# Start-up of a two-layer pooling and retention trunk: the adaLN stream opens the queue, and the second norm's transposes move ahead of its column

## The chip, the cores and the metric

One Trainium2 chip, one core. The metric is device microseconds of one execution. The kernel before takes 2433.22 us, the median of 3 runs (2433.15 to 2435.69).

## The reference, cut to what matters

x is 256 tokens by 2048 channels; everything is float32. There are two layers. Each has a mixer (causal pooling in layer 0, retention in layer 1) and a squared-ReLU MLP with 8192 hidden channels. In front of each of these four stands an RMSNorm whose result is scaled and shifted by rows that are computed from the conditioning vector c, and behind each a gate row computed in the same way. These rows are called adaLN rows here.

```python
cond = jax.nn.silu(c)
for i in range(DEPTH):
    mod = jnp.einsum('bd,sdk->bsk', cond, ada_w[i]) + ada_b[i]
    shift_t, scale_t, gate_t = jnp.split(mod[:, 0], 3, axis=-1)
    shift_m, scale_m, gate_m = jnp.split(mod[:, 1], 3, axis=-1)
    h = modulate(rmsnorm(x, norm_g[i, 0]), shift_t, scale_t)
    ...
    x = x + gate_t[:, None, :] * y
    h = modulate(rmsnorm(x, norm_g[i, 1]), shift_m, scale_m)
    x = x + gate_m[:, None, :] * sq_relu_mlp(h, mlp_w1[i], mlp_w2[i])
return rmsnorm(x, final_g)
```

## The kernel before, in words

Five engines run their own programs, written out by hand in the order in which each executes them, and meet in semaphores. Every large load is issued by SP, in order, on one queue. A load that has to wait for its buffer holds back all that stand behind it.

**adaLN pieces.** The weights of the adaLN rows come in pieces of 128 rows by 1024 columns (512 KB). A segment is 32 pieces: segments 0, 1 and 2 are shift, scale and gate of the pooling mixer, segment 3 is the lower half of shift and scale of the first MLP, segment 4 the upper half. Pieces 0 to 15 of a segment make its first 1024 columns and pieces 16 to 31 the other 1024. Segments 0 to 4 use 12 buffers in turn (`ada_raw` 4, `ada_early_h` or `ada_early_a` 8), so piece n may be loaded once piece n-12 has been used. A table says who uses a piece (`ON_PE`): the DVE multiplies it by its column of `cond` and adds it to `ada_acc` (L1346, L1349), or TensorE multiplies it into a PSUM bank (L689). In front of the last piece of each sixteen, TensorE adds what the DVE has summed (`row_blocks`, L664) and waits for `ada_done` to do so.

**From a segment to a norm.** The ACT copies the bank to `seg_row` (L1082), TensorE transposes it to columns (`column`, L747), the DVE adds the bias (L1446) and makes the gain (L1606). The normed x of the first MLP comes from TensorE: `norm_fill(f)` (L785) multiplies two of the 16 channel blocks of x by a diagonal matrix of the tokens' inverse root mean squares, which transposes and scales them at once, into bank `tb`. There are eight fills. `norm_evac` (L1017, called from `norm_bank`) evacuates one with gain and shift into a small buffer `hbuf`, and the DVE splits it into `h_hi` and `h_lo` (`split_h`, L1617 and L1619).

**The products.** Each float32 product is made of three passes: weights are split by the ACT into `w_hi` (L972, `hi`) and by the DVE into `w_lo` (L1340, `lo`). A chunk is 256 rows by 512 columns of weights (512 KB, four buffers), 12 matmuls of 128x512 on TensorE (L555). Here the first MLP starts with 28 chunks (`p1`, seven parts of four) that need only the lower half of the normed x, while segment 4 is still being loaded, and goes on with the upper half (`h1`).

**Order of the work around the change.** SP: eight small tables (c, norm gains, identity, four of biases, `rcount`), four pieces, x, then pieces, with pool weights and two MLP chunks in between (behind pieces 25 and 27 of segment 3), then two more chunks, then chunks and segment 4's pieces in turn. The ACT queue issues `bias_row` and `scale_row` first, each one row copied to 128 partitions. POOL loads the MLP's gate bias (a row of 2048 copied to 128 partitions, 1 MB written) as soon as x holds the mixer's result. TensorE makes fills 0 and 1 behind piece 15 of segment 3, and fills 2 to 7 each ahead of a chunk of the MLP.

## Time and profile before

| | before |
|---|---|
| timed runs | 2433.22 us (2433.15 to 2435.69) |
| profiled execution's own time | 2431.67 us |
| its span | 2429.8 us |
| TensorE busy | 2347.9 us, 97% |
| VectorE (DVE) busy | 1573.0 us, 65% |
| ScalarE (ACT) busy | 1082.4 us, 45% |
| mean of the DMA | 256 GB/s |

The span runs from the first instruction to the last; the execution's own time is 1.9 us longer. Times in all rows are microseconds from the span's start. TensorE's busy share says that most of the span is matmuls. Its first twelfth is another stage: there the DMA engines are busy all the time and TensorE is not. The change lies in that stage and at its end.

### The profile page before, as it was taken

How to read it: one execution, taken by the hardware profiler on the slowest of the kernel's cores; microseconds unless marked ns; L12 is line 12 of the kernel's file. 1: busy time of each engine (PE TensorE's matmuls, PEld its weight loads, DVE VectorE, ACT ScalarE, POOL GpSimd, SP SyncE). 2: the span in 40 equal slices, each digit the busy share in tenths (PEclk: the TensorE clock that was granted, in tenths of full speed). 3: DMA queues.
4: the chain of work that ended last, by engine and by line, in shares of the span. 5: the costliest groups of instructions: out<-in, count | busy, mean ns of one | idle time of the engine just before them, and what ended most of it. 6: DMA issues, size and time to landing. Idle time of an engine off the chain costs nothing.

```text
span 2429.8 us, 30034 instructions
## 1 busy us (share of the span) xinstructions
PE 2347.9 (97%) x10421; PEld 1857.0 (76%) x10421; DVE 1573.0 (65%) x1646; ACT 1082.4 (45%) x1346; POOL 21.7 (1%) x30
## 2 busy tenths in 40 slices
PE   5778999999999999999999999999999999999998
PEld 1235788888888887888888888887788888888886
DVE  4567787676676888657566656566876444445455
ACT  1323454443443545444444444455543443443443
POOL 0000000000000000000000000000000000000000
PEclk8789999999999999999999999999999999999999
DMA  9999889887887986766766766666987656656654
GB/s 369 406 392 373 323 291 326 300 291 251 292 301 254 321 318 201 263 220 224 229 212 226 248 212 225 219 224 198 330 289 239 186 186 192 185 187 194 187 182 155
DMA packets 269404, 620.89 MB, mean 256 GB/s; under 512 B 19064, under 2 KB 19400, under 8 KB 268360
## 3 DMA queue, kind: packets, MB, share of 16 engines
q1 hardware_dynamic: 268112, 612.65, 74.6%
q0 software_dynamic: 880, 5.77, 0.7%
q8 instruction: 90, 1.47, 0.2%
q10 hardware_dynamic: 264, 0.52, 0.1%
q14 instruction: 58, 0.48, 0.1%
HBM read 616.77 MB, written 2.10 MB: 255 GB/s over the span
## 4 chain that ended last, share of the span: by engine, by line
PE 91%; DMA 4%; DVE 3%; issue 1%; ACT 1%; SPq 1%; POOL 0%; ACTq 0%; POOLq 0%; DVEq 0%
PE acc L555 85%; DMA ada_early_h<-in_ada_w 3%; PE tb L656 2%; PE mod_ps L689 1%; PE score_ps L689 1%; DVE ada_acc L1346 0%; DMA ada_raw<-in_ada_w 0%; DVE w_lo L1340 0%; PE score_ps L906 0%; PE tb L785 0%; SPq L399 0%; DVE h_lo L1534 0%; PE mod_ps L664 0%; PE score_ps L664 0%; PE acc L916 0%
## 5 line engine op out<-in xcount | busy, mean ns | idle before, releaser
L1340 DVE TENSOR_TENSOR w_lo<-raw,w_hi 128x1024 fp32r<-128x1024 f32 x776 | 947.0, 1224 | 735.3 <-ACT w_hi L972 735.2
L972 ACT ACTIVATE w_hi<-raw 128x1024 fp32r<-128x1024 f32 x776 | 822.0, 1060 | 1167.8 <-PE acc L555 1096.8
L555 PE MATMUL acc<-w_hi,h_lo 128*128 128x512 f32 x1792 | 706.4, 394 | 8.6 <-DVE h_lo L1534 5.7
L555 PE MATMUL acc<-w_hi,h_hi 128*128 128x512 f32 x1792 | 698.0, 390 | 0.0
L555 PE MATMUL acc<-w_lo,h_hi 128*128 128x512 f32 x1792 | 697.4, 389 | 0.0
L555 PE MATMUL acc<-w_hi,a_lo 128*128 128x512 f32 x1312 | 516.5, 394 | 0.0
L555 PE MATMUL acc<-w_hi,a_hi 128*128 128x512 f32 x1312 | 511.1, 390 | 0.0
L555 PE MATMUL acc<-w_lo,a_hi 128*128 128x512 f32 x1312 | 510.7, 389 | 0.0
L555 PEld LDWEIGHTS acc<-w_hi,h_lo 128*128 128x128 f32 x1792 | 336.5, 188 | 86.3 <-issue 7.9
L555 PEld LDWEIGHTS acc<-w_hi,h_hi 128*128 128x128 f32 x1792 | 336.4, 188 | 70.5
L555 PEld LDWEIGHTS acc<-w_lo,h_hi 128*128 128x128 f32 x1792 | 336.7, 188 | 68.8 <-issue 1.4
L1346 DVE SCALAR_TENSOR_TENSOR ada_acc<-ada_raw,cond,ada_acc 128x1024 f32<-128x1024 f32 x238 | 304.3, 1279 | 17.0 <-DMA ada_raw<-in_ada_w 16.8
L555 PEld LDWEIGHTS acc<-w_hi,a_lo 128*128 128x128 f32 x1312 | 246.6, 188 | 60.2 <-issue 8.5
L555 PEld LDWEIGHTS acc<-w_lo,a_hi 128*128 128x128 f32 x1312 | 246.7, 188 | 52.2 <-issue 1.9
L555 PEld LDWEIGHTS acc<-w_hi,a_hi 128*128 128x128 f32 x1312 | 246.4, 188 | 51.9
L988 ACT ACTIVATE ev<-acc 128x512 f32<-128x512 f32 x121 | 64.6, 584 | 7.7 <-PE acc L555 6.4
L1346 DVE SCALAR_TENSOR_TENSOR ada_acc<-ada_early_h,cond,ada_acc 128x1024 f32<-128x1024 f32 x36 | 46.2, 1284 | 32.4 <-DMA ada_early_h<-in_ada_w 32.1
L1582 DVE TENSOR_TENSOR a_lo<-tb,a_hi 128x512 fp32r<-128x512 f32 x80 | 51.3, 682 | 0.0
L689 PE MATMUL mod_ps<-ada_early_h,cond 128*32 128x512 f32 x88 | 31.6, 814 | 17.9 <-DMA ada_early_h<-in_ada_w 17.9
L1003 ACT ACTIVATE sq_junk<-x 128x512 bf16<-128x512 f32 x46 | 28.4, 618 | 35.1 <-DVE x L1495 16.8
L993 ACT ACTIVATE a_hi<-tb 128x512 fp32r<-128x512 f32 x80 | 42.7, 586 | 0.0
L1227 ACT ACTIVATE ev<-ev 128x512 f32<-128x512 f32 x64 | 36.7, 627 | 0.0
(162 smaller groups left out, 759.2 us busy)
## 6 DMA issues: line engine op xcount, KB each, us to landing
raw<-in_mlp_w SPq DMA_DIRECT2D x512, 512.0 KB, 4.4
ada_raw<-in_ada_w SPq DMA_DIRECT2D x280, 512.0 KB, 5.8
raw<-in_ret_w_in SPq DMA_DIRECT2D x192, 512.0 KB, 3.9
ada_early_h<-in_ada_w SPq DMA_DIRECT2D x84, 512.0 KB, 13.1
raw<-in_ret_w_out SPq DMA_DIRECT2D x64, 512.0 KB, 4.1
ada_early_a<-in_ada_w SPq DMA_DIRECT2D x20, 512.0 KB, 9.9
raw<-in_pool_w SPq DMA_DIRECT2D x8, 512.0 KB, 12.5
x<-in_x SPq DMA_DIRECT2D x2, 1024.0 KB, 11.3
```

The lines of the kernel that those rows point to most:

```text
L555: mm = nc.tensor.matmul(acc[pair][t][:], l[:, CK * c + j, tok], w[:, c % RING, j, :], start=first and j == 0 and i == 0, stop=last and j = ...
L656: tr = nc.tensor.transpose(tb[b][:, j * S + t * P:j * S + (t + 1) * P], source(t)[:, m * P:(m + 1) * P], ident[:])
L689: mm = nc.tensor.matmul(bank[32 * b:32 * b + 32, :], cond[:, k:k + 1].to_broadcast([P, 32]), raw_rows[:, b % 2 * NB:(b % 2 + 1) * NB], sta ...
L972: nc.scalar.activation(w_hi[:, o % RING], raw[:, o % RING], ACT.Copy).then_inc(hi_ready, 1)
L988: nc.scalar.activation(target[:, t, :], acc[pair][t][:], func).then_inc(evac, 1)
L993: nc.scalar.activation(targets, tb[b][:].rearrange("p (k t) -> p k t", k=2), ACT.Copy).then_inc(tevac, 1)
L1003: nc.scalar.activation(sq_junk[:, t, :], x[:, t, block_ * NB:(block_ + 1) * NB], ACT.Square, accum_out=ssq[:, t, block_:block_ + 1]).then_ ...
L1227: nc.scalar.activation(ev[:, u % 2, t, :], ev[:, u % 2, t, :], ACT.Square).then_inc(sq_done, 1)
L1340: nc.vector.tensor_tensor(w_lo[:, o % RING], raw[:, o % RING], w_hi[:, o % RING].bitcast(F32), ALU.subtract).then_inc(lo_ready, 1)
L1346: nc.vector.scalar_tensor_tensor(out=part, in0=raw_rows, scalar=cond[:, k:k + 1], in1=part, op0=ALU.mult, op1=ALU.add).then_inc(ada_done, 1)
L1582: nc.vector.tensor_tensor(a_lo[:, k:k + 2, :], tb[b][:].rearrange("p (k t) -> p k t", k=2), a_hi[:, k:k + 2, :].bitcast(F32), ALU.subtract ...
```

## The change

Six edits.

1. SP no longer issues the small tables. Its queue opens with the first four adaLN pieces. The ACT queue issues the tables, in the order c, identity, then behind the silu of c: `rcount`, norm gains, four of biases, the two gate rows. TensorE and the DVE take c first (`cond`), and norm gains and biases some pieces later.
2. `bias_row` and `scale_row` are zeroed by POOL and loaded as 4 rows of 512 on partitions 0, 32, 64 and 96, not copied to 128.
3. All eight fills of the MLP's norm stand ahead of its column, between pieces 15 and 24 of segment 3. The ACT copies each bank as it is to scratch (`transposed_x`), in two new buffers `xT`. Gain and shift are applied later, in place: channel blocks 0 and 1 by the DVE (`modulate_first`), the others by the ACT (`norm_bank`).
4. Who uses a piece changes in segment 3: in its first sixteen TensorE has 11 pieces for 9, in the other sixteen 5 for 9.
5. One MLP chunk is loaded within segment 3 (behind piece 29) for two, and the three others of the first four behind its end.
6. POOL's load of the gate bias waits until the upper half of the norm has been split (`h_ready`), since `xT` lies where it lands.

```diff
-LAST_PE = (1, 3, 5, 7, 9, 11, 13, 14, 15)
+LOW_SHIFT_PE = (1, 3, 4, 5, 7, 8, 9, 11, 12, 13, 15)
+LOW_SCALE_PE = (1, 3, 7, 11, 15)
...
+        xT = [scratch[:, 0:2048].rearrange("p (k t) -> p k t", k=KT // 2),
+              scratch[:, 6144:8192].rearrange("p (k t) -> p k t", k=KT // 2)]
...
-                if a in (25, 27):
-                    load_chunk(a // 2 - 12, first_part(a // 2 - 12))
+                if a == 29:
+                    load_chunk(0, first_part(0))
...
             pe.wait_ge(gate_ready, 4)
-            norm(2)
-            shared_rows(3, 16, SEG)
+            pe.wait_ge(diag_ready, 1)
+            for f in range(KT // 2):
+                norm_fill(f)
+                if f % 2:
+                    shared_rows(3, 15 + f, 17 + f)
+            shared_rows(3, 24, SEG)
             column(score_ps)
...
+            def transposed_x(f):
 
                 act.wait_ge(tr_done, n.of("TB") + 1)
+                k = 2 * f % (KT // 2)
+                nc.scalar.activation(xT[f // 4][:, k:k + 2, :], tb[f % 2][:].rearrange("p (k t) -> p k t", k=2),
+                                     ACT.Copy).then_inc(tevac, 1)
...
-            act.dma_start(bias_row[:], by_block(gate_bias)).then_inc(bias_in, 16)
...
+            act.wait_ge(rows_zero, 1)
+            act.dma_start(rows[0:KT, 1, :], c_in.rearrange("b (k p) -> (b k) p", p=P)).then_inc(cond_in, 16)
+            act.dma_start(ident[:], ident_in).then_inc(const_in, 16)
+            act.wait_ge(cond_in, 16)
             nc.scalar.activation(rows[:, 1, :], rows[:, 1, :], ACT.Silu).then_inc(cond_rows, 1)
+            act.dma_start(rcount[:], rcount_in).then_inc(rcount_loaded, 16)
...
+            act.dma_start(bias_row[0:P:32, :], gate_bias.rearrange("(b n) -> b n", b=4)).then_inc(bias_in, 16)
...
+            for f in range(KT // 2):
+                transposed_x(f)
             hi(0)
+            copy_rows(score_ps, 2, PE_BEFORE[4 * SEG])
+            norm_bank(1)
             hi(1)
-            copy_rows(score_ps, 2, PE_BEFORE[4 * SEG])
-            norm_bank(0)
-            norm_bank(1)
+            norm_bank(2)
             hi(2)
-            norm_bank(2)
+            norm_bank(3)
             hi(3)
...
             lo(0)
-            lo(1)
             take_half(0)
             gains(slice(0, KT // 2))
+            modulate_first()
             split_h(0)
             split_h(1)
+            lo(1)
+            split_h(2)
             lo(2)
...
-            pool.wait_ge(x_added, 4 * TT)
+            pool.wait_ge(h_ready, CH)
             load_gate_bias(mlp_gate, 1, mlp_bias_in)
```

The instruction order shows three places. First SP's opening, before:

```order
L452 DMA rows<-in_c 16x128 [waits rows_zero]
L453 DMA rows<-in_norm_g 64x128
L454 DMA ident<-in_ident 128x128
L457 DMA rows<-in_ada_b 32x128 x4
L458 DMA rcount<-in_rcount 128x64
L399 DMA ada_raw<-in_ada_w 128x1024 x4
```

and now, where L407 is the line of the pieces' loads:

```order
L407 DMA ada_raw<-in_ada_w 128x1024 x4
L462 DMA x<-in_x 128x2048 x2
L407 DMA ada_early_h<-in_ada_w 128x1024 x8
L407 DMA ada_raw<-in_ada_w 128x1024 [waits ada_done]
L407 DMA ada_raw<-in_ada_w 128x1024 [waits ada_rows_multiplied]
```

The pieces stand first and wait for nothing. Second, TensorE at the end of segment 3, from its last piece on, before (L747 is the column, L785 a fill, L555 the first MLP chunk):

```order
L689 MATMUL score_ps<-ada_early_h,cond 32x512 [waits ada_in7]
L689 MATMUL score_ps<-ada_early_h,cond 32x512
L747 MATMUL score_ps<-ident,seg_row 128x128 [waits mod_col_ready,seg_row_ready]
L747 MATMUL score_ps<-ident,seg_row 128x128 x3
L785 MATMUL tb<-diag,x 128x128 [waits tr_bank_evacuated,lo_ready]
L785 MATMUL tb<-diag,x 128x128 x3
L555 MATMUL acc<-w_hi,h_lo 128x512 [waits evac_done,h_ready]
```

and now, from fills 6 and 7 (L783) on, with pieces 23 and 27, the sum of the DVE's share (L662) and piece 31 ahead of the column (L745):

```order
L783 MATMUL tb<-diag,x 128x128 [waits tr_bank_evacuated]
L783 MATMUL tb<-diag,x 128x128 x3
L687 MATMUL score_ps<-ada_early_h,cond 32x512 [waits ada_in11]
L687 MATMUL score_ps<-ada_early_h,cond 32x512
L687 MATMUL score_ps<-ada_raw,cond 32x512 [waits ada_in3]
L687 MATMUL score_ps<-ada_raw,cond 32x512
L662 MATMUL score_ps<-ada_acc,ones 32x512 [waits ada_done]
L662 MATMUL score_ps<-ada_acc,ones 32x512
L687 MATMUL score_ps<-ada_early_h,cond 32x512 [waits ada_in7]
L687 MATMUL score_ps<-ada_early_h,cond 32x512
L745 MATMUL score_ps<-ident,seg_row 128x128 [waits mod_col_ready,seg_row_ready]
L745 MATMUL score_ps<-ident,seg_row 128x128 x3
```

No fill stands between the column and the MLP's chunks any more. Third, the DVE behind the column (L1446), before:

```order
L1340 TENSOR_TENSOR w_lo<-raw,w_hi 128x1024 [waits hi_ready] x2
L1446 TENSOR_TENSOR mod_col<-score_ps,bias_col 128x2x8 [waits col_transposed]
L1606 SCALAR_TENSOR_TENSOR gain_col<-mod_col,norm_col 128x8 [waits mod_col_ready]
L1617 CAST h_hi<-scratch 128x512 [waits tr_bank_evacuated]
L1619 TENSOR_TENSOR h_lo<-scratch,h_hi 128x512 [waits h_hi_done]
```

and now:

```order
L1340 TENSOR_TENSOR w_lo<-raw,w_hi 128x1024 [waits hi_ready]
L1446 TENSOR_TENSOR mod_col<-score_ps,bias_col 128x2x8 [waits col_transposed]
L1606 SCALAR_TENSOR_TENSOR gain_col<-mod_col,norm_col 128x8 [waits mod_col_ready]
L1617 TENSOR_SCALAR scratch<-scratch,gain_col,mod_col 128x256 [waits tr_bank_evacuated,gain_ready]
L1617 TENSOR_SCALAR scratch<-scratch,gain_col,mod_col 128x256
L1630 CAST h_hi<-scratch 128x512 [waits first_two_modulated]
L1632 TENSOR_TENSOR h_lo<-scratch,h_hi 128x512 [waits h_hi_done]
```

One of two splits of weights has moved from in front of the column to behind the second split of h, and the DVE applies the first gain and shift itself.

## Rows read from the trace of the kernel before

**Rows 1.** The page: span, and DMA's busy tenths in 40 slices of 61 us.

```profile
span 2429.8 us, 30034 instructions
...
DMA  9999889887887986766766766666987656656654
```

**Rows 2.** Busy time by stage: length, engines, granted clock, DMA share, GB/s.

```profile
0.00:5.00 5.00, 0.00 (x0) 0.00 (x0) 0.00 (x0) 1.28 (x1) 0.81 (x7) 1.00 0.23 65
5.00:10.00 5.00, 0.00 (x0) 0.00 (x0) 0.00 (x0) 0.31 (x1) 0.00 (x0) 1.00 0.84 247
...
175.00:180.00 5.00, 2.99 (x8) 0.55 (x8) 4.13 (x8) 0.36 (x2) 2.32 (x2) 0.50 0.93 322
195.00:200.00 5.00, 4.74 (x12) 1.06 (x14) 2.58 (x3) 0.00 (x0) 0.00 (x0) 0.52 1.04 397
240.00:260.00 20.00, 20.00 (x89) 15.62 (x88) 16.11 (x14) 9.09 (x11) 0.00 (x0) 1.00 1.04 399
```

**Rows 3.** Timeline of the opening: start, length, engine, line, and idle time before.

```profile
1.19 0.39 SPq L452 DMA_DIRECT2D rows<-in_c  x1
5.25 1.96 SPq L399 DMA_DIRECT2D ada_raw<-in_ada_w  x4
6.51 0.31 ACT L1096 ACTIVATE rows<-rows 128x128 f32<-128x128 f32 x1 [2.70 <-DMA rows<-in_norm_g]
...
17.04 0.75 DVE L1349 TENSOR_SCALAR ada_acc<-ada_raw,cond 128x1024 f32<-128x1024 f32 x1
20.18 0.63 ACT L1003 ACTIVATE sq_junk<-x 128x512 bf16<-128x512 f32 x1 [13.36 <-DMA x<-in_x]
```

**Rows 4.** Timeline, TensorE on pieces 5 and 7 of segment 0.

```profile
22.77 1.92 PE L689 MATMUL mod_ps<-ada_early_h,cond 128*32 128x512 f32 x4 [5.62 <-DMA ada_early_h<-in_ada_w]
25.32 1.92 PE L689 MATMUL mod_ps<-ada_early_h,cond 128*32 128x512 f32 x4 [0.63 <-DMA ada_early_h<-in_ada_w]
```

**Rows 5.** Timeline of segment 3: piece 14, SP, the DVE's sum, POOL's load, fills, piece 30.

```profile
168.01 1.05 PE L689 MATMUL score_ps<-ada_raw,cond 128*32 128x512 f32 x4 [0.23 <-DMA ada_raw<-in_ada_w]
164.41 11.62 SPq L399 DMA_DIRECT2D ada_early_h<-in_ada_w  x8
177.01 1.92 PE L664 MATMUL score_ps<-ada_acc,ones 128*32 128x512 f32 x4 [7.95 <-DVE ada_acc L1346]
177.47 0.69 POOL L1955 DMA_DIRECT2D scratch<-in_ada_b  x1
180.57 3.06 PE L785 MATMUL tb<-diag,x 128*128 128x128 f32 x16
196.54 0.13 PEld L689 LDWEIGHTS score_ps<-ada_early_h,cond 128*32 128x32 f32 x2 [1.09 <-DMA ada_early_h<-in_ada_w]
```

**Rows 6.** Timeline from segment 3's row to the MLP's first chunk.

```profile
201.22 0.60 ACT L1082 ACTIVATE seg_row<-score_ps 128x512 f32<-128x512 f32 x1 [7.48 <-PE score_ps L689]
204.48 0.69 DVE L1619 TENSOR_TENSOR h_lo<-scratch,h_hi 128x512 fp32r<-128x512 f32 x1
205.73 1.03 ACT L1017 ACTIVATE scratch<-tb,mod_col,gain_col 128x256 f32<-128x256 f32 x2
205.23 0.50 PE L555 MATMUL acc<-w_hi,h_lo 128*128 128x512 f32 x1
```

**Rows 7.** Chain that ended last, through the MLP's first chunks: start, length, what.

```profile
217.31 1.11 PE tb L785 x8
218.42 2.75 PE acc L555 x12
...
222.15 1.09 PE tb L785 x8
...
297.21 0.89 PE tb L785 x8
```

**Rows 8.** Timeline of the DVE: fourth split of h, fifth split of weights.

```profile
210.28 0.43 DVE L1617 CAST h_hi<-scratch 128x512 fp32r<-128x512 f32 x1 [0.71 <-ACT scratch L1017]
215.99 1.22 DVE L1340 TENSOR_TENSOR w_lo<-raw,w_hi 128x1024 fp32r<-128x1024 f32 x1
```

More of the change, by code:

```diff
@@ L575, in unit, with half_unit @@
                     n.unit(kind)
-            def half_unit(kind, pair, before, after, c0, free):
+            def half_unit(kind, pair, after, c0, free):
                 for o in range(HALF):
                     pe.wait_ge(lo_ready, n.of("U") * HALF + (o + 1))
-                    for hook in before.get(o, []):
-                        hook()
                     ready_h(c0 + o)
@@ L845, in _ @@
             for i in range(PARTS):
-                before, after = {}, {}
-                if i < 2:
-                    before = {o: [lambda f=2 * i + o + 2: norm_fill(f)] for o in range(2)}
+                after = {}
                 for o in range(HALF):
@@ L877, in group @@
                             elif part_of(layer, first, u) is not None:
-                                before = {}
-                                if (first, u) == (0, 0):
-                                    before = {o: [lambda f=6 + o: norm_fill(f)] for o in range(2)}
-                                half_unit("h1", u % 2, before, hooks, HALF, last_but_one if first == 0 else mlp_free(u))
+                                half_unit("h1", u % 2, hooks, HALF, last_but_one if first == 0 else mlp_free(u))
                             elif u < 4:
```

127 lines of the change are left out of this document (68 added, 59 removed).

## The prediction

> **What bounds the kernel now.** First the page. The span is 2429.8 us, and the DMA engines are full in the first four slices and half to three quarters busy later [rows 1]. Then busy time by stage: from 240 us on TensorE is busy 20.00 of 20 us [rows 2]. So behind the start-up every microsecond of the chain is TensorE's, and what the change does there counts only where it takes work from TensorE. Ahead of it the chain waits for pieces. Two pieces that TensorE multiplies one after the other, with one of the DVE's between, are 2.55 us apart [rows 4]: 1.28 us for each 512 KB, 410 GB/s. From about 8 us until the last piece of segment 3 the queue sets the pace, then a chain of small steps leads to the MLP's first chunk at 205.23 us [rows 6]. The time of the kernel is the moment of that chunk plus what TensorE does behind it. The change has four terms, each a shift of one part of this.
>
> **1. The opening.** SP issues c at 1.19 us and the first piece only at 5.25 us [rows 3]; now the piece is issued where the wait on POOL's zeroes used to begin, at about 0.75 us, the issue 4.5 us sooner. The DMA engines have a share of 0.23 in the first 5 us and 0.84 in the next [rows 2], and x, 4 pieces' and 2 MB's worth of transfers behind SP's first load, has landed at 20.18 us [rows 3]. Up to there the engines gave 0.23 x 5 + 0.84 x 5 + 10.2 = 15.5 us, of which the two gate rows copied to 128 partitions (2 x 256 KB) are 1.3. The remaining 14.2, less the 3% by which a full share exceeds 1, is 13.8; it now starts near 2.3 us and ends near 16.1. That is 4.1 us sooner, and I take 4.2. The small tables now compete with the stream instead of standing ahead of it, which is in the 13.8. Bounds: 3.0 if they hold the engines a microsecond longer, 5.5 if most of them are as cheap as their bytes. Who uses the first pieces must keep up: the silu comes 5.3 us after the issue of c, and the DVE takes piece 0 at 17.04 us, 10.5 behind the silu [rows 3]; in these 10.5 lie a wait for tables and, about half, band arithmetic that needs `rcount`, which is now issued behind the silu. With the silu at 4.5 to 6 us and the same 10.5 behind it, piece 0 is taken at 15 to 16.5. The 12 buffers and x (12 x 1.28 + 5.1 from 2.3 on) keep the engines busy until about 23 us, so there are 6 to 8 us of cover.
>
> At the first row a rule of the Trainium skill can be weighed ("DMA: Bandwidth & Descriptors", section "Issuing engines are not separate DMA queues"): loads issued from several engines run on the same 16 engines and interleave, and only the sequencer's issue time is saved. By it this term would be the 4.5 us of issue and the sum 15.1 instead of 14.8.
>
> **2. Segment 3** (times here without the shift of term 1). Piece 14 has landed at 168.01 us and piece 30 at 196.54 [rows 5]: 28.5 us for 16 pieces and two chunks, which at 1.28 us are 23.0. The other 5.5 us are two things. POOL's gate bias at 177.47 us [rows 5] writes 1 MB, two pieces' worth, 2.6 us. And SP needs 11.62 us for eight pieces from 164.41 us on [rows 5], because pieces 4, 6, 8 and 10 are freed by the DVE, one between each two gated blocks of x; the engines run dry (0.93 and 322 GB/s in 175 to 180 us [rows 2]), 2.9 us. All three go. The bias leaves the stage. One chunk, 1.3 us, moves behind piece 31, where it has 6 us before TensorE needs it. TensorE takes pieces 4, 8 and 12, so only 6 and 10 stand between gated blocks: pieces 16 to 25 can be issued by about 168 us and keep the queue full until 182. Piece 30 then comes 17 transfers, 21.8 us, behind piece 14: 6.7 us sooner.
>
> What could block SP now is TensorE, whose fills are in front of pieces 17, 19 and 23. Two cold fills take 3.06 us [rows 5]. The DVE is done with piece 14 3.1 us sooner than with 12 before (two pieces less on its path, no waiting for the last square), so the sum of its share starts near 173.9 instead of 177.01 and the fills near 177. Piece 17 is used by 181, piece 19 by 184 to 185, the last fill ends by 188; pieces 29 and 31 wait for the first two and have backlog until 186 and 190. This is why I take the full term. Bounds: 3.8 (bias and chunk alone) and 7.2.
>
> **3. From piece 30 to the row.** Before: 196.54 to 201.22, 4.7 us [rows 5, 6]. Now piece 30 is the DVE's, 1.28 us, and then come the sum and piece 31 on TensorE. Cold they take 180.57 - 177.01 = 3.6 us [rows 5], at full clock half, 1.8. So 3.2 to 4.9: a gain of 1.5 to a loss of 0.2. The granted clock is 0.52 in 195 to 200 us [rows 2], in a stretch before which TensorE had little; with the fills it has more work, until about 189, but only two pieces in the last 8 us. I take a gain of 0.5, nearer cold.
>
> **4. From the row to the end.** The first h_lo starts at 204.48, lasts 0.69 and is followed by the first matmul at 205.23 [rows 6]. In its chain the ACT's 1.03 us for two blocks [rows 6] becomes two DVE operations of 256 columns, estimated at 0.5 from a 0.75 us operation of 1024 columns [rows 3]: 0.5 sooner. Then the fills leave TensorE: those before chunks 1 and 4 (0.89 and 1.11), 5 (1.09) and the one at 297.21 (0.89) [rows 7]; the other two lay beside the DVE's split. But chunk 4 needs the DVE's fifth w_lo. Before it started at 215.99 [rows 8] and chunk 4 at 218.42, behind the fill [rows 7]. Now one more w_lo (1.13 from start to start) stands in that order, the pause of about 0.8 in front of the fourth split [rows 8] and 0.5 of modulation go: 215.8, ready at 217.0. TensorE would be there at 215.7 and stalls 1.3 us. Chunk 4 gains 1.4, and with 1.09 and 0.89 the term is 3.4. Later the DVE needs 2.5 us a chunk (one w_lo and 1.1 pieces at 1.2) against TensorE's 2.75 [rows 7] and 0.16 of pieces, and does not fall behind again. Bounds: 2.1 (a stall again at chunk 5 or a cold first chunk) and 4.7 (no stall).
>
> The eight plain copies on the ACT, each at most the 1.03 us of two blocks [rows 6], lie beside TensorE's pieces. The gate bias lands near 290 us, long before the last unit of the MLP's first round reads it, while the engines are 7 to 8 tenths busy [rows 1]. Neither costs anything; without cover the load would be 2.6 us.
>
> **Sum.** 4.2 + 6.7 + 0.5 + 3.4 = 14.8 us. The span goes to 2415.0, the profiled execution's own time to 2416.9. The median of the runs is 1.55 above that of the profiled one (2433.22 against 2431.67), so 2418.4 us. The bounds sum to 8.8 and 18.9: 2414.3 to 2424.4.
>
> **The rivals.** *The clock.* TensorE idles before the row and the MLP starts at half speed. What is cold at 0.50 to 0.52 takes twice as long; the first chunk's 2.85 us would be 5.7, of which the 1.3 of stall hide as much, and term 3 is a loss of 0.2: 2.3 us worse, 2420.7. For it, the clock before; against it, the fills. *Fills hold the queue.* If the diagonals come 5 us later than I reckon, SP waits for pieces 17 and 19 and the dry time returns in another place: term 2 is 3.8, the time 2421.3. *Late setup.* If c and `rcount` each take 12 us behind the stream, the band arithmetic (half of the 10.5 us) ends near 31, and the engines stand 9 to 10 us: 2428. Against this the Trainium skill has a rule (the same page, section "Queues, rings and completion order"): each engine takes turns between the queues that have work. No row here shows two full queues at once. *The other side:* the same mechanism at its worst. The kernel is slower only when the DVE's first piece comes 20 us later than the backlog allows, which needs more than 16.6 us for each of the two loads one after the other; at 18 us each it is 2436 to 2438. In the trace x, queued behind four pieces, took 13 us. *No gain in term 4,* the MLP's start being held by weights: 2421.8.
>
> **How the numbers follow.** Forecast 0.50, clock 0.14, fills 0.14, term 4 0.07, late setup 0.10, slower 0.03, and 0.02 for a gain above 19 us. Within 0.2% (4.9 us, about what a measurement can tell) are the worse half of late setup, 0.05, so faster 0.92, same 0.05, slower 0.03. The range runs from the lower bound with a little for the forecast's own error, 2413.5, to 2425.5, which leaves out most of late setup.
>
> **What would show it.** Piece 0 issued under 1 us, x landed near 16; the DVE's piece 0 near 15; pieces 16 to 25 of segment 3 issued without 3 us gaps; the MLP's first matmul near 193.3 (205.23 - 4.2 - 6.7 - 0.5 - 0.5); a stall of TensorE ahead of chunk 4 on w_lo; no L785 row behind the column. The prediction is wrong if the DMA share falls below 1.0 between 15 and 190 us, or if segment 3's last piece waits for TensorE.

## The result and the profile after

The changed kernel takes 2422.12 us (median of 5 runs, 2419.99 to 2422.18), the kernel before in the same session 2434.18 us (median of 5): a ratio of 0.9947, with a 95% interval of 0.9932 to 0.9961, 12.06 us less. The forecast was 14.8 us less, 2418.4 us. The profiled executions are 9.5 us apart (spans 2429.8 and 2420.3).

To see where the time went, two moments are compared in every kernel below: when ACT copies the row of segment 3, which ends the stage that waits for transfers, and when TensorE begins the first transposes of the MLP's activations, which every kernel here reaches by the same work behind the row, but for what was changed. In the kernel before the second moment is this row of the timeline (start, length):

```profile
314.28 0.92 PE L656 MATMUL tb<-ident,ev 128*128 128x128 f32 x7
```

and in the changed kernel this one:

```profile
303.11 1.03 PE L654 MATMUL tb<-ident,ev 128*128 128x128 f32 x8
```

That is 11.17 us sooner. The page of the changed kernel answers to [rows 1]:

```profile
span 2420.3 us, 30026 instructions
...
DMA  9999988887887986776766766766987666666654
```

The busy time by stage answers to [rows 2] (start and end, length, then busy time of PE, PEld, DVE, ACT and POOL with the number of instructions, granted clock, DMA share, GB/s):

```profile
0.00:5.00 5.00, 0.00 (x0) 0.00 (x0) 0.00 (x0) 1.34 (x2) 1.73 (x9) 1.00 0.61 201
5.00:10.00 5.00, 2.62 (x7) 0.74 (x9) 0.17 (x1) 0.25 (x1) 0.00 (x0) 1.00 1.05 420
175.00:180.00 5.00, 5.00 (x35) 3.08 (x34) 4.86 (x5) 1.87 (x4) 0.00 (x0) 1.00 1.03 407
195.00:200.00 5.00, 5.00 (x17) 3.87 (x17) 4.93 (x8) 4.26 (x7) 0.00 (x0) 0.69 0.79 259
280.00:285.00 5.00, 3.07 (x11) 2.12 (x10) 3.31 (x6) 4.94 (x9) 0.00 (x0) 0.85 0.59 224
285.00:290.00 5.00, 5.00 (x20) 4.05 (x19) 3.02 (x5) 2.28 (x4) 0.00 (x0) 0.81 0.64 210
```

The transfers start sooner (0.61 and 1.05 in the first two windows, where 0.23 and 0.84 stood), and the dry stretch of segment 3 is gone (1.03 and 407 GB/s at 175 to 180 us, where it was 0.93 and 322). But behind the row TensorE has two stretches below its full clock, 0.69 at 195 to 200 us and 0.85 and 0.81 at 280 to 290 us. The timeline of the opening answers to [rows 3]:

```profile
0.74 1.83 SPq L407 DMA_DIRECT2D ada_raw<-in_ada_w  x4
1.20 0.40 ACTq L1084 DMA_DIRECT2D rows<-in_c  x1
4.94 0.31 ACT L1087 ACTIVATE rows<-rows 128x128 f32<-128x128 f32 x1 [1.55 <-DMA rows<-in_c]
12.48 0.17 DVE L1653 MEMSET scratch<- 128x128 f32 x1 [4.74 <-DMA rcount<-in_rcount]
14.43 0.63 ACT L998 ACTIVATE sq_junk<-x 128x512 bf16<-128x512 f32 x1 [9.18 <-DMA x<-in_x]
17.50 0.75 DVE L1349 TENSOR_SCALAR ada_acc<-ada_raw,cond 128x1024 f32<-128x1024 f32 x1
```

x is there at 14.43 us instead of 20.18. The DVE's piece 0 at 17.50 is not sooner but 0.46 later. The timeline of segment 3 and of what follows answers to [rows 5, 6]:

```profile
159.49 5.10 SPq L407 DMA_DIRECT2D ada_early_h<-in_ada_w  x8
186.15 1.28 DVE L1346 SCALAR_TENSOR_TENSOR ada_acc<-ada_early_h,cond,ada_acc 128x1024 f32<-128x1024 f32 x1 [1.31 <-DMA ada_early_h<-in_ada_w]
190.85 0.60 ACT L1072 ACTIVATE seg_row<-score_ps 128x512 f32<-128x512 f32 x1 [5.00 <-PE score_ps L687]
...
194.63 0.68 PE L555 MATMUL acc<-w_hi,h_lo 128*128 128x512 f32 x1 [2.47 <-issue]
205.68 1.22 DVE L1340 TENSOR_TENSOR w_lo<-raw,w_hi 128x1024 fp32r<-128x1024 f32 x1
```

SP issues its eight pieces in 5.10 us and not 11.62. Piece 30, now the DVE's (186.15), comes 10.4 us sooner than before, the row 10.37, the MLP's first matmul 10.60. The chain that ended last answers to [rows 7] (start, length, what):

```profile
192.16 2.47 issue
194.63 15.49 PE acc L555 x60
...
277.23 0.44 PE score_ps L745 x4
277.67 2.75 PE acc L555 x12
280.41 1.93 issue
282.35 20.92 PE acc L555 x84
```

No fill stands in it any more. In their place are 60 matmuls in 15.49 us, which at the pace of the 12 in 2.75 us would take 13.8, and at 280.41 us a wait of 1.93 us behind the second column, in front of 84 matmuls that take 20.92 us and not 19.3. So from the row to the transposes only 0.8 us is gained (113.06 us before, 112.26 now), although all the fills left.

Of the 11.17 us the profiled execution shows 1.7 less at its end. One piece of that is a gap in the second round of the MLP, where neither code nor order changed: the chain there reads `601.40 0.84 issue`. The medians, 12.06 us apart, don't show such a loss, and I count it to the scatter of single executions.

### The profile page after: what moved, and what is told of

It is laid out like the page before. It is cut to its first block, busy times and chain, and to the rows that moved or that the text cites. A ratio compares the mean times of both kernels' runs of the same rounds, so it can differ in the third digit from the quotient of the medians.

```text
span 2420.3 us, 30026 instructions
## 1 busy us (share of the span) xinstructions
PE 2343.5 (97%) x10413; PEld 1857.8 (77%) x10413; DVE 1576.8 (65%) x1650; ACT 1087.0 (45%) x1352; POOL 22.2 (1%) x32
## 4 chain that ended last, share of the span: by engine, by line
PE 91%; DMA 4%; DVE 3%; issue 1%; ACT 0%; SPq 0%; POOL 0%; ACTq 0%; POOLq 0%; DVEq 0%
PE acc L555 85%; DMA ada_early_h<-in_ada_w 3%; PE tb L654 2%; DMA ada_raw<-in_ada_w 1%; PE mod_ps L687 1%; DVE w_lo L1340 1%; DVE ada_acc L1346 1%; PE score_ps L901 0%; DVE h_lo L1534 0%; PE mod_ps L662 0%; DMA raw<-in_ret_w_in 0%; DMA rcount<-in_rcount 0%; PE score_ps L687 0%; PE acc L911 0%; PE acc L912 0%
## 5 line engine op out<-in xcount | busy, mean ns | idle before, releaser
L555 PE MATMUL acc<-w_hi,h_lo 128*128 128x512 f32 x1792 | 707.3, 395 | 14.6 <-issue 7.8
L555 PE MATMUL acc<-w_hi,h_hi 128*128 128x512 f32 x1792 | 699.1, 390 | 0.0
L555 PE MATMUL acc<-w_lo,h_hi 128*128 128x512 f32 x1792 | 698.8, 390 | 0.0
L555 PE MATMUL acc<-w_hi,a_lo 128*128 128x512 f32 x1312 | 516.6, 394 | 0.0
L555 PE MATMUL acc<-w_hi,a_hi 128*128 128x512 f32 x1312 | 511.2, 390 | 0.0
L555 PE MATMUL acc<-w_lo,a_hi 128*128 128x512 f32 x1312 | 511.0, 389 | 0.0
L555 PEld LDWEIGHTS acc<-w_hi,h_lo 128*128 128x128 f32 x1792 | 337.2, 188 | 94.0 <-issue 15.6
L555 PEld LDWEIGHTS acc<-w_hi,h_hi 128*128 128x128 f32 x1792 | 337.1, 188 | 70.8
L555 PEld LDWEIGHTS acc<-w_lo,h_hi 128*128 128x128 f32 x1792 | 337.4, 188 | 69.2 <-issue 1.4
L555 PEld LDWEIGHTS acc<-w_hi,a_lo 128*128 128x128 f32 x1312 | 246.6, 188 | 60.4 <-issue 8.6
L555 PEld LDWEIGHTS acc<-w_lo,a_hi 128*128 128x128 f32 x1312 | 246.7, 188 | 52.4 <-issue 1.9
L555 PEld LDWEIGHTS acc<-w_hi,a_hi 128*128 128x128 f32 x1312 | 246.5, 188 | 51.9
```

The source lines that it names most:

```text
L555: mm = nc.tensor.matmul(acc[pair][t][:], l[:, CK * c + j, tok], w[:, c % RING, j, :], start=first and j == 0 and i == 0, stop=last and j = ...
```

## The experiments

Twelve kernels, each timed 5 or 11 times with the kernel before beside it. The changed kernel was timed in another session than they were, and the medians of the kernel before differ by up to 1 us between sessions, so a difference of that size between two medians of this table says nothing. The moments are in us of each profiled execution; "row to transposes" is their difference.

| kernel | median | ratio, 95% interval | row copied | first transposes | row to transposes |
|---|---|---|---|---|---|
| before | 2433.2 to 2434.2 | 1 | 201.22 | 314.28 | 113.06 |
| changed | 2422.12 | 0.9947 (0.9932 to 0.9961) | 190.85 | 303.11 | 112.26 |
| 1 opening only | 2428.50 | 0.9980 (0.9971 to 0.9989) | 195.69 | 308.82 | 113.13 |
| 2 gate bias later only | 2430.42 | 0.9989 (0.9980 to 0.9998) | 198.53 | 311.62 | 113.09 |
| 3 segment 3 only | 2429.70 | 0.9986 (0.9977 to 0.9995) | 196.38 | 310.80 | 114.42 |
| 4 all but the fills | 2423.72 | 0.9961 (0.9947 to 0.9974) | 190.37 | 304.78 | 114.41 |
| 5 column sooner | 2417.17 | 0.9934 (0.9920 to 0.9947) | 190.49 | 298.83 | 108.34 |
| 6 extra matmuls | 2420.72 | 0.9945 (0.9932 to 0.9959) | 190.21 | 302.83 | 112.62 |
| 7 the same, fifth w_lo first | 2418.90 | 0.9939 (0.9925 to 0.9953) | 190.50 | 302.41 | 111.91 |
| 8 rcount sooner | 2420.04 | 0.9945 (0.9932 to 0.9959) | 189.80 | 301.96 | 112.16 |
| 9 as 7, extra matmuls fitted | 2416.43 | 0.9931 (0.9918 to 0.9945) | 189.80 | 298.83 | 109.03 |
| 10 as 9, column sooner | 2413.36 | 0.9917 (0.9904 to 0.9931) | 189.61 | 296.48 | 106.87 |
| 11 wide gate rows on ACT | 2430.54 | 0.9986 (0.9977 to 0.9995) | 199.95 | 311.85 | 111.90 |
| 12 wide gate rows on SP | 2430.53 | 0.9988 (0.9979 to 0.9997) | 197.62 | 309.68 | 112.06 |

### 1 to 4. The parts of the change one by one

My theory was that the terms of the sum stand apart from each other and that the last of them, the fills, had been eaten by the clock. The rival was that one full queue hides or moves part of the gains.

The first takes over the hunks of the diff on the opening alone (SP's first loads, the tables on ACT's queue, the gate rows as 4 rows, the transposes in two steps):

```diff
-            sp.wait_ge(rows_zero, 1)
-            sp.dma_start(rows[0:KT, 1, :], c_in.rearrange("b (k p) -> (b k) p", p=P)).then_inc(rows_in, 16)
...
             for a in range(RING):
                 load_early(0, a)
```

> The kernel before with the opening of the change alone (SP starts with pieces, the tables on ACT's queue, gate rows as 4 rows). My theory: the 4.2 us of term 1 arrive whole and stay, as every later transfer waits in one full queue: x 5.6 us sooner, the copy of the MLP's row by ACT at 197.0 us instead of 201.22, the kernel 4 us faster. Rival 1: part of the changed kernel's gain at the opening belongs to later parts; then the row is copied at 198.5 or later. Rival 2: the segment 3 is bound by SP, which waits for the DVE, and not by bytes; the DVE runs the same steps 4.2 us sooner, so this one also gives 197.0, but the windows from 170 to 185 us would then have no share below 1.

The row comes at 195.69 us, 5.53 sooner, and the median is 4.7 us lower. The gain arrives whole and stays, but it is larger than my term. Not all of it is the opening's: in the chain the last wait for a transfer ends at 190.44 us and not at 195.26, 4.8 us sooner, and the other 0.7 is TensorE's steps from there to the row, 5.3 us where the kernel before took 6.0, with nothing changed in them (the sum alone took 0.86 us, 1.37 before). The dry time is still there, also in this run (0.93 and 318 GB/s at 170 to 175 us), so it was not swallowed by it.

The second is the kernel before with one line changed:

```diff
-            pool.wait_ge(x_added, 4 * TT)
+            pool.wait_ge(h_ready, CH)
             load_gate_bias(mlp_gate, 1, mlp_bias_in)
```

> The kernel before with POOL's 1 MB load of the MLP's gate bias moved behind the MLP's h, and nothing else. My theory: its bytes are worth 2.6 us of a full queue, and the dry time behind the gated blocks stays as it is: row copied at 198.6 us instead of 201.22, DMA share still below 1 in 170 to 185 us. Rival: SP, held by the DVE, was the bound there, and the bias only filled the hole that SP leaves; then the share falls further in that stretch and the row comes less than 1 us sooner.

The row comes 2.69 us sooner, the bytes' 2.6. That the two agree so closely is luck in part: in this execution the DVE's first gated block of x came 0.7 us later than before (162.62 and 161.90 us), and TensorE's steps behind the last wait for a transfer took 0.5 us less, with nothing changed in either. The stretch stays dry, as the busy time by stage of this run shows (columns as above):

```profile
175.00:180.00 5.00, 2.27 (x6) 0.56 (x8) 4.13 (x8) 1.08 (x4) 1.68 (x1) 0.50 0.92 324
180.00:185.00 5.00, 5.00 (x26) 2.97 (x23) 4.58 (x4) 0.00 (x0) 0.00 (x0) 0.69 0.95 313
```

So the bias and SP's wait for the DVE are two separate losses.

The third adds to the second the table of pieces, the DVE's order and the chunk behind piece 29:

```diff
+PE_OF = [EARLY_PE] * 6 + [LOW_SHIFT_PE, LOW_SCALE_PE] + [LATE_PE] * 2
...
-                if a in (25, 27):
-                    load_chunk(a // 2 - 12, first_part(a // 2 - 12))
+                if a == 29:
+                    load_chunk(0, first_part(0))
...
-            early(3, 4, 6)
+            early(3, 4, 8)
             gated(1)
-            early(3, 6, 8)
+            early(3, 8, 11)
             gated(2)
-            early(3, 8, 10)
             gated(3)
```

> The kernel before with the three changes to segment 3: which pieces TensorE takes and the DVE's order around the gated blocks, one chunk behind piece 29 where two stood at 25 and 27, the gate bias later. Fills and opening as before. My theory: the whole of term 2, 6.2 us (piece 30 at 190.3, row copied at 195.0), of which 2.6 are in the run with the bias alone. Rival: the order of the DVE and TensorE gives nothing by itself, because the dry time is refilled by backlog later; then the row is copied at about 197.3 (bias and chunk, 3.9).

First a line of its busy time by stage, then its piece 30 in the timeline of the DVE:

```profile
175.00:180.00 5.00, 5.00 (x24) 2.99 (x20) 4.34 (x7) 0.00 (x0) 1.15 (x1) 0.66 1.02 406
```

```profile
191.34 1.28 DVE L1348 SCALAR_TENSOR_TENSOR ada_acc<-ada_early_h,cond,ada_acc 128x1024 f32<-128x1024 f32 x1 [1.30 <-DMA ada_early_h<-in_ada_w]
```

The queue is full now (406 GB/s), and piece 30 comes at 191.34, 5.2 us sooner than the 196.54 of before [rows 5]. That is more than the bias's 2.7 and less than the 6.2 expected of this run and the 6.7 of the forecast. The row is only 4.84 us sooner and the transposes only 3.48: with more of TensorE's pieces at the front of the segment, it has less to do at its end, and the granted clock is 0.59 and 0.50 in 185 to 195 us. The steps behind piece 30 take 5.04 us (4.7 before), and 1.36 us more go by from the row to the transposes. The chain shows where these are. The fill behind the column takes 1.83 us and not 1.13, and the first chunk 3.66 and not 2.98. This is the chunk in the kernel before and in this run:

```profile
205.26 2.98 PE acc L555 x12
...
201.13 3.66 PE acc L557 x12
```

The granted clock in 200 to 205 us is 1.00 in the kernel before and 0.70 here. In the kernel before and in runs 1 and 2 the first chunk runs at full clock; in the changed kernel and in runs 3, 4, 5, 8, 11 and 12, all with the new order of segment 3 and without extra matmuls, it does not. So the cold start of the MLP comes with the new order of segment 3 and not with the fills.

The fourth is the changed kernel without the hunks on the fills (the function `norm` back, `hbuf` in place of `xT`, no `modulate_first`):

```diff
-            for f in range(KT // 2):
-                norm_fill(f)
-                if f % 2:
-                    shared_rows(3, 15 + f, 17 + f)
+            norm(2)
+            shared_rows(3, 16, SEG)
```

> The changed kernel without its fills ahead: opening and segment 3 as changed, but the second norm's fills, the ACT's modulation and the DVE's split as before (two fills ahead of the column, the others in front of chunks 1 and on). My theory: the row is copied at 190.9 as in the changed kernel, or up to 0.7 later since TensorE has less work ahead of it; TensorE's first chunk is 0.3 to 0.5 us later behind the row; and the fills cost their 4 us in the MLP's first round but hide the clock's loss and the idle of 1.93 us at the second column, so that the first transposes of the MLP come at 316 (changed: 315.05): the fills' removal is worth 1 us and not 3.4. Rival: it is worth the 3.4 of term 4, what the changed kernel lost to the clock having another cause, and the transposes come at 318.4.

Row at 190.37, transposes at 304.78. Against this run the changed kernel needs 2.15 us less from the row to the transposes, where I had said 1 us here and 3.4 in the forecast. This is not yet what the fills are worth at like clocks: both kernels start the first chunk cold, but only the changed kernel also has the 0.85 and 0.81 behind the second column (this run: 1.00 from 280 to 300 us). And against the kernel before both runs with the new segment 3 and the old fills (3 and 4) need 1.35 us more behind the row, which is the cold start again (here the fill takes 2.05 us and the first chunk 3.43). Together, 2.15 - 1.35 is the 0.8 us of the changed kernel.

### 5. The second column sooner

```diff
-                    after[HALF - 2] = [lambda: column(score_ps)]
+                    after[HALF - 3] = [lambda: column(score_ps)]
...
-                    if (i, s) == (PARTS - 1, HALF - 1):
+                    if (i, s) == (PARTS - 1, HALF - 2):
                         take_half(1)
```

and one step sooner on ACT as well (`copy_rows`, `norm_bank(4)`, `norm_bank(5)`).

> The changed kernel with the MLP's second column one chunk sooner on TensorE (behind chunk 1 of the last part and not behind chunk 2), the copy of its row one chunk sooner on ACT, and column, gains, modulation and split one chunk sooner on DVE and ACT. My theory: the 1.93 us for which TensorE waits at 280.41 us are the way from the column to the first split, behind a w_lo that the DVE takes first, and the granted clock of 0.85 and 0.81 in 280 to 290 us follows from that idle time: both go, 1.93 + 1.6 us, the first transposes of the MLP come at 299.6 us instead of 303.11. Rival 1: the clock falls there for a reason of its own; then only the idle goes, 301.2. Rival 2: TensorE then waits for the weights of the next chunk instead, and no more than 0.5 us is gained.

The chain that ended last, behind the second column:

```profile
274.02 0.44 PE score_ps L745 x4
274.46 24.53 PE acc L555 x108
298.99 0.87 PE tb L654 x8
```

In this chain of run 5 108 matmuls follow the column in one stretch at full clock, and the way from the row to the transposes is 3.92 us shorter (3.5 expected). The median falls by 5 us. The wait and the low clock behind it are gone together, as in my theory, but runs 9 and 11 below show that the second does not always follow the first.

### 6, 7 and 9. Keeping TensorE's clock

```diff
+            def keep_warm(count):
+                for _ in range(count):
+                    nc.tensor.matmul(acc[0][0][:, 0:S], ones[:], x[:, 0, 0:S], start=True, stop=True)
...
-            shared_rows(3, 24, SEG)
+            shared_rows(3, 24, SEG - 1)
+            pe.wait_ge(evac, 4 * TT)
+            keep_warm(8)
+            shared_rows(3, SEG - 1, SEG)
+            keep_warm(3)
             column(score_ps)
+            keep_warm(8)
```

> The changed kernel with 19 matmuls of 128x256 on TensorE whose result nobody reads, 8 ahead of the last sum of segment 3, 3 behind its last piece, 8 between the column and the first chunk of the MLP. My theory: they keep the clock at its full level, the row's two steps take 1.7 us instead of 3.4 and the row is copied at 189.4 us instead of 190.85, and the first chunk takes 2.85 us instead of 4.4. But then chunk 4 stands for 1.2 us for the DVE's fifth w_lo, as term 4 of the prediction had it, and of the 3.0 us 1.8 are left: first transposes at 301.3 instead of 303.11. Rival 1: no stall at chunk 4, 300.1. Rival 2: the clock does not come back for them, and nothing is gained or 0.5 us lost.

The granted clock is 1.00 in every window from 180 to 205 us, but the eight matmuls ahead of the sum take 3.65 us and not the 1.8 that I had reckoned, and the sum and the first chunk wait for them: first matmul at 195.15, 0.5 later than without. The row is copied at 190.21 us and the transposes come at 302.83, where 189.4 and 301.3 were expected. And the stall of term 4 appears. In the chain of this run chunk 4 hangs on the DVE's fifth w_lo:

```profile
203.02 1.29 DVE ada_acc L1356
204.38 1.17 issue
205.55 1.23 DVE w_lo L1350
206.82 3.01 PE acc L555 x12
```

The next run lets the DVE take that w_lo first:

```diff
             for i in range(PARTS):
                 for s in range(HALF):
+                    if (i, s) == (0, 0):
+                        lo(s + LEAD)
                     early(4, late_pieces(HALF * i + s + LEAD - 1), late_pieces(HALF * i + s + LEAD))
```

> The kernel of the run with the extra matmuls, and the DVE takes its fifth w_lo ahead of the four pieces of segment 4 that stand in front of it. My theory: the fifth w_lo is ready by 201 us, the stall ahead of chunk 4 goes, and the first transposes come at 300.1 us, 1.2 us sooner than without. Rival: chunk 5 or 6 then waits, since the four pieces stand in front of the sixth w_lo; then the two runs are within 0.4 us.

The transposes come at 302.41 us, not at 300.1. From the row to the transposes this run needs 0.71 us less than run 6, between the 1.2 and the 0.4 of the two views. The stall existed, and was smaller than I had said (about 0.7 us, since run 6 began its first chunk 0.5 us late). Then the counts are fitted, 4, 1 and 5 in place of 8, 3 and 8:

> The kernel with the extra matmuls and the fifth w_lo taken first, with 4, 1 and 5 extra matmuls in place of 8, 3 and 8: each lasted 0.46 us and not the 0.23 that I had reckoned, so that 8 of them pushed the sum of segment 3 back by 1 us and the first chunk by 1 us. My theory: the clock stays full and nothing is pushed back; from the DVE's piece 30 (186.15 in the changed kernel) the row is copied 3.2 us later and not 4.7, the first chunk begins at 193.2 us and is warm, and the first transposes come at 299.8 us instead of 303.11. Rival: with fewer matmuls the clock falls as in the changed kernel; then 302 to 303.

The transposes come at 298.83 us, 4.28 sooner than in the changed kernel where 3.3 was expected, and the median is 5.7 us lower. In the chain of this run:

```profile
193.58 13.86 PE acc L555 x60
...
277.76 1.91 issue
279.67 19.32 PE acc L555 x84
```

The first 60 matmuls take 13.86 us instead of 15.49: the cold start had cost 1.63 us. Behind the wait of 1.91 us, which is as long as before, 84 matmuls take 19.32 us instead of 20.92, at a clock of 1.00 (changed kernel: 0.85 and 0.81):

```profile
280.00:285.00 5.00, 5.00 (x23) 4.10 (x22) 4.02 (x5) 4.31 (x8) 0.00 (x0) 1.00 0.51 147
285.00:290.00 5.00, 5.00 (x24) 4.14 (x23) 3.71 (x6) 2.12 (x2) 0.69 (x1) 1.00 0.94 276
```

Nothing was changed there. Run 11 below, which has no extra matmuls and a cold first chunk, shows the same:

```profile
290.77 1.91 issue
292.69 19.33 PE acc L555 x84
```

So the same wait of 1.90 to 1.93 us costs 1.6 us more in five executions (the changed kernel and runs 6, 7, 8 and 12, 84 matmuls in 20.91 to 20.93 us) and nothing more in two (runs 9 and 11). Not all that run 9 gains is then owed to the extra matmuls. The 1.63 us at the first chunk are: without them the 60 matmuls took 15.31 to 16.73 us (changed kernel, runs 5, 8, 11 and 12), with them 13.62 to 13.88 (runs 7, 9 and 10). The 1.6 us behind the column are not, since run 11 is spared them without extra matmuls and runs 6 and 7 lose them with more, and the 1.05 us at the row can be scatter, as the next run shows.

### 8. rcount sooner

```diff
             act.dma_start(ident[:], ident_in).then_inc(const_in, 16)
+            act.dma_start(rcount[:], rcount_in).then_inc(rcount_loaded, 16)
             act.wait_ge(cond_in, 16)
             nc.scalar.activation(rows[:, 1, :], rows[:, 1, :], ACT.Silu).then_inc(cond_rows, 1)
-            act.dma_start(rcount[:], rcount_in).then_inc(rcount_loaded, 16)
```

> The changed kernel with rcount issued behind the identity and ahead of ACT's wait for c, where it stood behind the silu. My theory: the DVE's piece 0 is taken at 14 to 15 us instead of 17.5 and SP's thirteenth load is issued as much sooner, but the 12 buffers and x keep the engines busy until 22 us anyway: no difference beyond 0.5 us at the row (190.85) and in the time. Rival: the late setup cost the changed kernel part of its opening; then the row comes 1 us sooner or more.

The timeline of the DVE, its piece 0 of segment 0 and its piece 30 of segment 3:

```profile
14.10 0.75 DVE L1349 TENSOR_SCALAR ada_acc<-ada_raw,cond 128x1024 f32<-128x1024 f32 x1
...
186.46 1.28 DVE L1346 SCALAR_TENSOR_TENSOR ada_acc<-ada_early_h,cond,ada_acc 128x1024 f32<-128x1024 f32 x1 [1.31 <-DMA ada_early_h<-in_ada_w]
```

Piece 0 is taken at 14.10, 3.4 us sooner than in the changed kernel, and piece 30 at 186.46, not sooner (186.15). The setup had cover, as my theory said. The row did come 1.05 us sooner, which is the rival's number, but not by its way: from piece 30 to the row this execution took 3.34 us and the changed kernel's 4.70, as TensorE's sum and last piece ran at full clock here (1.05 and 0.88 us) with nothing changed ahead of them. Between executions this step thus varies by up to 1.7 us: 3.34 here, 4.70 in the changed kernel, 5.05 in run 5. The median is 2.1 us under the changed kernel's where no more than 0.5 was expected, but the times of the two overlap (2418.66 to 2422.59 here, 2419.99 to 2422.18), so a gain in time is neither shown nor excluded.

### 10. Both together

> The same with the second column one chunk sooner as well. My theory: both losses to the clock and both idle times are apart from each other, so the gains add: 3.3 and 3.9 us, first transposes at 295.9 us instead of 303.11, the kernel 7 us under the changed kernel, near 2415 us. Rival: the MLP's second half then waits for weights or for partial sums, which the sooner start does not move; then less than 5 us of the 7.

Two lines of the chain of this run:

```profile
193.39 13.88 PE acc L555 x60
...
272.10 24.54 PE acc L555 x108
```

The transposes come at 296.48 us, 6.6 sooner than in the changed kernel (7.2 expected), and the median is 2413.36 us: 8.8 us under the changed kernel and 0.83% under the kernel before (ratio 0.9917, 0.9904 to 0.9931). It is the fastest of all. Alone, each of the two changes brought the transposes 4.28 us forward, together 6.6 and not 8.6: the 1.6 us of clock behind the second column are in both.

### 11 and 12. The gate rows to 128 partitions

```diff
-            act.dma_start(bias_row[0:P:32, :], gate_bias.rearrange("(b n) -> b n", b=4)).then_inc(bias_in, 16)
+            act.dma_start(bias_row[:], gate_bias.rearrange("(b o n) -> b o n", b=4, o=1).to_broadcast([4, 32, NB])).then_inc(bias_in, 16)
```

and the same for `scale_row`, in their place on ACT's queue behind the stream's first loads.

> The changed kernel with the gate bias and the pool scale loaded to 128 partitions as before (2 x 256 KB instead of 2 x 8 KB). My theory: their bytes are worth 1.3 us in the full queue of the opening: x lands 1.3 us later, the row is copied at 192.1 instead of 190.85. Rival: small packets of few bytes cost the engines as much as wide ones; then less than 0.3 us.

I was far off. x lands at 14.43 us as before, since the wide rows stand behind it, but the row is copied 9.1 us later, at 199.95, and the gain of the changed kernel is nearly gone (2430.54). Two loads of 256 KB cost not 1.3 us but 8 to 9. The busy time by stage of run 11 shows how:

```profile
25.00:30.00 5.00, 1.93 (x6) 0.18 (x4) 1.28 (x1) 0.00 (x0) 0.00 (x0) 0.50 1.03 331
30.00:35.00 5.00, 1.78 (x6) 0.19 (x4) 1.28 (x1) 0.00 (x0) 0.00 (x0) 0.50 1.02 331
```

And this is the changed kernel in the first of the two stretches:

```profile
25.00:30.00 5.00, 2.84 (x8) 0.20 (x6) 2.52 (x3) 0.00 (x0) 0.00 (x0) 0.75 1.02 408
```

The engines' share is as full as ever, but they move 331 GB/s instead of 408. The last run puts the wide rows into SP's own queue, behind the twelfth piece, to see whether it is two queues taking turns that costs:

```diff
+            sp.wait_ge(gate_rows_zero, 1)
+            sp.dma_start(bias_row[:], gate_bias.rearrange("(b o n) -> b o n", b=4, o=1).to_broadcast([4, 32, NB])).then_inc(bias_in, 16)
+            sp.dma_start(scale_row[:], pool_scale.rearrange("a (b o n) -> (a b) o n", b=4, o=1).to_broadcast([4, 32, NB])).then_inc(scale_in, 16)
             for a in range(EARLY, SEG):
                 load_early(0, a)
```

> The changed kernel with both gate rows loaded to 128 partitions, but by SP behind the twelfth piece, in the queue of the stream itself, and not by ACT beside it. With the wide rows on ACT's queue the row was copied at 199.95 us instead of 190.85, and the engines moved 303 to 350 GB/s at a full share from 20 to 35 us. Theory 1: it is the taking turns between two queues that costs, packets of one queue in between those of the other; in one queue the 2 x 256 KB cost their bytes, 1.3 us, and the row is copied at 192.1 us. Theory 2: reading the same 2 KB 32 times over is slow by itself wherever it stands; then the row is copied at 199 to 200 again. I hold the first for likelier, 0.6 to 0.4.

Its busy time in the same stretch, and then two lines of the DVE's timeline:

```profile
25.00:30.00 5.00, 1.05 (x4) 0.14 (x4) 0.00 (x0) 0.00 (x0) 0.00 (x0) 0.68 1.04 258
```

```profile
34.84 1.28 DVE L1349 SCALAR_TENSOR_TENSOR ada_acc<-ada_raw,cond,ada_acc 128x1024 f32<-128x1024 f32 x1 [9.87 <-DMA ada_raw<-in_ada_w]
194.27 1.28 DVE L1349 SCALAR_TENSOR_TENSOR ada_acc<-ada_early_h,cond,ada_acc 128x1024 f32<-128x1024 f32 x1 [1.31 <-DMA ada_early_h<-in_ada_w]
```

The DVE stands 9.87 us for a piece behind them, and its piece 30 comes at 194.27, 8.1 us later than in the changed kernel; the row is copied at 197.62, only 6.8 later, since TensorE's steps behind piece 30 ran at full clock here (3.35 us). The theory of two queues, which I had held for likelier, falls: such a load is slow in either of the two queues. The Trainium skill has a rule on its shape ("DMA: Bandwidth & Descriptors", section "Rules for kernel authors"): a transfer is spread over the engines by the slowest of its dimensions, and an outermost dimension of fewer than 16 confines it to as many engines. Here the outermost is 4. By it, an estimate: 512 KB on 4 engines, each with a sixteenth of 410 GB/s, are 5.1 us. The trace agrees in the direction, but the loss is 8 to 9 us and the mean share of the 16 engines stays at 1.02 to 1.04, which does not look like 12 idle ones. Whether it is that or the 32 reads of the same 2 KB is open: no run here separates them. One measurement speaks against the reads: POOL's load of the gate bias reads one 8 KB row 128 times, and by run 2 it cost 2.7 us, its bytes.

## Why the prediction was nearly right

The kernel became faster by nearly what was forecast, inside the range, by the mechanisms named, and with errors that cancel only in part.

**The opening** (term 1, 4.2 us): 5.5 us by run 1, of which 4.8 are transfers and 0.7 steps of TensorE that happened to run faster; 6.0 as the difference of the rows of runs 3 and 4. The start of the stream was forecast well (0.74 against about 0.75, x landed at 14.43 against near 16). Undersized was the price of the two wide gate rows, costed by bytes at 1.3 us: runs 11 and 12 show that behind a full stream they cost 8 to 9. In the kernel before they stood ahead of the stream, where the engines were half idle, so only part of that was to be gained. That the 0.6 us missing in the term (1.3 by the row) are theirs is argued, not shown. The rule of the Trainium skill that I had weighed there ("DMA: Bandwidth & Descriptors", section "Issuing engines are not separate DMA queues") says that only the issue time is saved. By it the term is 4.5 us, which lies nearer to the measured 4.8 than my 4.2; the scatter of 0.5 to 0.7 us between executions does not let the trace decide between the two.

**Segment 3** (6.7): 5.2 us by run 3. The gate bias is as forecast (2.7 by run 2, 2.6 in the sum). The chunk and the dry time, 4.2 in the sum, gave 2.5. The dry time is gone for good, by the windows. Of the missing 1.7 us, 0.4 is the dry time itself, which I had put at 2.9: the engines moved 371 GB/s from 168.00 to 196.50 us in the kernel before and 406 from 168.00 to 191.30 in run 3, and 28.5 x (1 - 371/406) is 2.5 us, an estimate from these rates. What the rest is was not taken apart further; up to 0.6 of it can be scatter, since in run 3 the DVE's first block of x stood at 162.45 us and in the kernel before at 161.90, with nothing changed ahead of it.

**From piece 30 to the row** (0.5): 4.70 us now, 4.7 before, no gain; the range of -0.2 to 1.5 covers what single executions showed (3.34 to 5.05), except the last of these.

**From the row to the end** (3.4): 0.8. This is the step that failed. The term took TensorE's clock for full (a cold first chunk stood only in its lower bound and among the rivals), and it counted the 0.89 us of the fill at the second column [rows 7] without asking what that fill covered. Apart from the clock its size was about right: run 9, at full clock in both places as the kernel before is, needs 109.03 us from the row to the transposes, 4.0 less than before (it also has the fifth w_lo first, about 0.7 us by runs 6 and 7, which the changed kernel did not need). The changed kernel loses 3.2 of these 4.0 us, in two places.

The first chunk ran cold, 1.63 us, which is the rival of the clock; its condition held and its price (2.3 with the row's) was about right. The cold start came with the new order of segment 3, as runs 3 and 4 show. That it comes from TensorE having less to do at the segment's end is argued, not shown: in runs 8 and 12 the sum and the last piece ran at full clock, and the first chunk still ran cold. It hid the stall ahead of chunk 4 that I had charged with 1.3 us: TensorE came late enough, and the stall appeared only in run 6, at about 0.7.

And one place I had not looked at: the second column. Two fills (1.13 us, at 293.07 us in the chain before, and the 0.89) and 0.69 us of idle time went there, but TensorE now waits 1.93 us for the second column's way over the DVE, ACT and DVE, and then runs 84 matmuls 1.6 us slower. From the last sum of segment 4 to the transposes, with the same 120 matmuls, the chain took 30.94 us before (283.50 to 314.44) and takes 31.71 now (271.56 to 303.27): 0.8 us longer, where 0.89 shorter was counted. In the kernel before TensorE was idle for 0.69 of the 5 us around the fill, at full clock:

```profile
290.00:295.00 5.00, 4.31 (x23) 3.27 (x22) 3.45 (x7) 3.42 (x7) 0.00 (x0) 1.00 0.93 311
```

**The rivals.** The clock's was the one that came true in part: its time was 2420.7 and the result is 2422.1. The fills didn't hold SP: the share is 1.02 or more from 15 to 190 us. Late setup did not cost: c took 3.7 us from issue to use and rcount about 7.5 (issued behind the silu, used at 12.48), not 12. The DVE's piece 0 was later than the 15 to 16.5 forecast, which run 8 shows to be covered. The slower side was far away, but runs 11 and 12 show a neighbour of it: with the rows left wide, the same reordering would have given 0.12 to 0.14% and not 0.5%. Of the signs that the prediction named, two did not come: the MLP's first matmul stood at 194.63 us and not near 193.3, and TensorE did not stall ahead of chunk 4. The lower bounds of the four terms add to 8.7 us, not 8.8, which changes nothing.

## What to carry to other kernels

When work that fills a gap is taken off the engine that bounds the kernel, look at every place where it stood: what remains there is a bare wait on a chain of small steps, and it cost the clock as well in five executions of seven. Look also at where a new division of work leaves an engine idle before its long stretch: with segment 3's the MLP started cold. Move the head of that chain (here a column) a chunk ahead in the same edit; run 5 was worth 3.9 us for moving hooks at four places, of which 1.6 is a loss to the clock that some executions don't have. A load that repeats a few rows over many partitions should be costed by a measurement and not by its bytes, and kept out of a full stream; and work that holds the clock must be sized by a measured duration of one, since 8 matmuls twice as long as reckoned ate all that they gave.

## What the runs showed of the hardware

- 2 x 256 KB that repeat four 2 KB rows over 128 partitions cost 8 to 9 us in a stream of 410 GB/s, in either of two queues, with the engines' share at 1.02 to 1.04 and 258 to 331 GB/s moved in the windows shown. As 2 x 8 KB they left the stream at 408. POOL's load of one 8 KB row to 128 partitions, 1 MB, cost 2.7 us, no more than its bytes.
- The same idle time of 1.9 us on TensorE was followed by a granted clock of 0.70 to 0.96 in five executions (the changed kernel, runs 6, 7, 8 and 12) and by 1.00 in two (runs 9 and 11). The difference was 1.6 us over 84 matmuls. The rows show no difference ahead of it that explains this, and it stays open.
- The MLP's first chunk ran at full clock in the kernel before and in runs 1 and 2 (12 matmuls in 2.98 to 3.02 us) and below it in all seven executions with the new order of segment 3 and no extra matmuls. Ten extra matmuls of 128x256 (4.6 us), 4, 1 and 5 of them in three gaps, kept it full in two of two kernels.
- A matmul of 128x256 in f32 took 0.46 us at full clock, two instructions of 0.23 in the trace.
- Executions of the same loads differ by 0.5 to 0.7 us in a moment late in the stage bound by transfers (the DVE's first gated block of x at 161.90, 162.45 and 162.62 us in three kernels with the same code up to it).
